# A three-block transformer kernel on one core: projection split, masked copies, norm gain and the order of a closing changed together

## The reference

```python
for layer in range(2):
    mix = dsa_mixer(h, ...) if layer == 0 else hgrn2_mixer(h, ...)
    h = layer_norm(ALPHA * h + mix, ...)
    h = layer_norm(ALPHA * h + swiglu(h, ...), ...)
# second block: rms norm, 16-head attention with relative bias, out-projection, gated conv feed-forward, rms norm
```

## Time and profile before

| what | us |
|---|---|
| median of 3 runs | 949.24 |
| lowest and highest run | 948.96, 949.47 |
| the profiled execution's own time | 951.03 |
| its span, first to last instruction | 949.0 |
| TensorE busy (matmul) in the span | 923.1 |
| VectorE busy | 590.3 |
| ScalarE busy | 457.8 |
| GpSimd busy | 156.0 |

### The profile page before, as it was taken

One profiled execution on the slowest core, in us unless ns is written; L12 is line 12 of the kernel. 1 busy time (PEld: TensorE's weight loads), 2 busy tenths in 40 slices (PEclk: granted clock), 3 DMA queues, 4 the chain that ended last, 5 costly groups with the idle time before them and its releaser, 6 DMA issues.

```text
span 949.0 us, 13816 instructions
## 1 busy us (share of the span) xinstructions
PE 923.1 (97%) x5667; PEld 760.8 (80%) x5667; DVE 590.3 (62%) x957; ACT 457.8 (48%) x609; POOL 156.0 (16%) x128
## 2 busy tenths in 40 slices
PE   8989999999999999899999999999999999999996
PEld 6867788888887997688888888878777788888885
DVE  5874774554648579978736456494223567777775
ACT  5775352433433443543425343345656465564653
POOL 3283300000005500013000000040355201010011
PEclk9999999999999999999999999999999999999999
DMA  8981466555646644245755555449432465555531
GB/s 292 208 163 46 148 228 198 179 179 192 204 143 217 221 147 166 92 131 178 245 178 179 192 199 185 164 158 320 133 134 89 155 207 185 185 178 178 180 130 45
DMA packets 104382, 164.98 MB, mean 174 GB/s; under 512 B 4011, under 2 KB 74714, under 8 KB 104320
## 3 DMA queue, kind: packets, MB, share of 16 engines
q1 hardware_dynamic: 101056, 152.61, 48.6%
q0 software_dynamic: 3264, 11.49, 5.6%
HBM read 159.89 MB, written 4.19 MB: 173 GB/s over the span
## 4 chain that ended last, share of the span: by engine, by line
PE 84%; DVE 8%; ACT 4%; DMA 1%; issue 1%; POOL 1%; SPq 0%; DVEq 0%; POOLq 0%; ACTq 0%
PE PG L1791 12%; PE PA L1791 12%; PE PG L1793 12%; PE PG L1792 12%; PE PA L1793 12%; PE PA L1792 11%; DVE wlo L600 1%; DVE work L1516 1%; ACT whi L591 1%; PE PG L1927 1%; PE TB L2379 1%; PE TB L2042 1%; PE TB L1947 1%; PE PA L2196 1%; PE PA L2195 1%
## 5 line engine op out<-in xcount | busy, mean ns | idle before, releaser
L600 DVE TENSOR_TENSOR wlo<-raw,whi 128x2048 fp32r<-128x2048 f32 (+1 forms) x124 | 288.9, 2346 | 65.5 <-ACT whi L591 65.4
L591 ACT ACTIVATE whi<-raw 128x2048 fp32r<-128x2048 f32 (+1 forms) x142 | 268.7, 1908 | 49.9 <-PE PA L1793 18.7
L1791 PE MATMUL PG<-whi,xlo 128*128 128x512 f32 x548 | 218.4, 399 | 0.3 <-DVE xlo L1098 0.2
L1793 PE MATMUL PG<-whi,xhi 128*128 128x512 f32 x548 | 214.1, 391 | 0.0
L1792 PE MATMUL PG<-wlo,xhi 128*128 128x512 f32 x548 | 213.9, 390 | 0.0
L1793 PEld LDWEIGHTS PG<-whi,xhi 128*128 128x128 f32 x548 | 103.1, 188 | 22.0
L1791 PEld LDWEIGHTS PG<-whi,xlo 128*128 128x128 f32 x548 | 103.2, 188 | 21.8 <-DVE wlo L1322 0.8
L1792 PEld LDWEIGHTS PG<-wlo,xhi 128*128 128x128 f32 x548 | 103.3, 189 | 20.1
L1791 PE MATMUL PA<-whi,xlo 128*128 128x512 f32 (+1 forms) x292 | 117.1, 401 | 1.8 <-DVE xlo L1098 1.3
L1793 PE MATMUL PA<-whi,xhi 128*128 128x512 f32 (+1 forms) x292 | 112.5, 385 | 0.0
L1792 PE MATMUL PA<-wlo,xhi 128*128 128x512 f32 (+1 forms) x292 | 112.2, 384 | 0.0
(11 more groups left out here) (289 smaller groups left out, 1175.3 us busy)
## 6 DMA issues: line engine op xcount, KB each, us to landing
raw<-in_ffn_w_gate SPq DMA_DIRECT2D x44, 512.0 KB, 4.0
raw<-in_ffn_w_up SPq DMA_DIRECT2D x44, 512.0 KB, 5.0
raw<-in_ffn_w_down SPq DMA_DIRECT2D x22, 1024.0 KB, 4.8
raw<-in_w_up SPq DMA_DIRECT2D x44, 512.0 KB, 4.6
raw<-in_hgrn_w_in SPq DMA_DIRECT2D x16, 1024.0 KB, 5.3
raw<-in_w_qkv SPq DMA_DIRECT2D x12, 1024.0 KB, 5.3
raw<-in_w_down SPq DMA_DIRECT2D x11, 1024.0 KB, 4.8
raw<-in_att_w_o SPq DMA_DIRECT2D x4, 1024.0 KB, 5.8
```

Of the source, the lines that this page charges most:

```text
L591: nc.scalar.activation(whi[:, g, 0:n_], raw[:, s, 0:n_], ACT.Copy).then_inc(S("w_hi"), 1)
L600: nc.vector.tensor_tensor(wlo[:, s, 0:n_], raw[:, s, 0:n_], whi[:, g, 0:n_].bitcast(F32), ALU.subtract).then_inc(S("w_lo"), 1)
L1791: mm(dst, xl[:, k, rows], whi[:, g, cols], start=first, stop=False)
L1793: return mm(dst, xh[:, k, rows], whi[:, g, cols], start=False, stop=last_)
```

## The change

It has six parts.

1. The first projection's units 0 and 1 carry columns 0 to 255 and 512 to 647 (392 columns, `FIRST`), unit 2 carries 256 to 511 (k and v whole, 256 columns).
2. The order of the beginning: the small constants are turned after the first and before the second half of iq; the query's turn comes ahead of them (event cq before c0); VectorE splits units 2 and 3 later; ScalarE takes the projection out before it rounds unit 3.
3. ScalarE rounds units U_AO+2 and U_AO+3 after pairs 2 and 4 instead of 0 and 1; U_F0+1 after the fourth group of outputs instead of before.
4. The first out-projection: tile 3 of U_AO+1 is left to between the closing's rows; tile 0 of U_AO+2 is done in the last pair; row 0 of the new h is turned inside row 1's last unit.
5. Masked copies take both heads of a bank and row at once.
6. The gain of the HGRN norm, now a value for each partition, scales the turned outputs in their rounding and split.

```diff
-SKIP, EARLY = 392, 256
-C_V, C_KI, C_WI, C_K = 248, 376, 504, 512
+EARLY, SKIP = 256, 512
+FIRST = EARLY + IN_COLS - SKIP
+C_KI, C_WI, C_K, C_V = 256, 384, 392, 520
...
-        for name, k in (("x", 4), ("c0", 2), ("cq", 1), ...
+        for name, k in (("x", 4), ("cq", 1), ("c0", 2), ...
...
+            def gained_hi(g):
+
+                e = ev["ho"] + g
+                turned(e)
+                act.wait_ge(S("gno"), 16)
+                ac.activation(flat(xhi[:, 2 * g:2 * g + 2, :]), TB[:, e % 2, :], ACT.Copy, scale=gno)\
+                  .then_inc(S("x_hi"), 1)
...
             hi(2)
-            hi(3)
-
-            act.wait_ge(S("ang"), 1)
-            ac.activation(trig.rearrange("p a b c -> p (a b c)"), ang.rearrange("p a b c -> p (a b c)"),
-                          ACT.Sin).then_inc(S("trig"), 1)
             full(1)
-            ac.activation(pin[:, :, 0:512], PG[:, :, :], ACT.Copy).then_inc(S("pin"), 1)
+            ac.activation(pin[:, :, 0:FIRST], PG[:, :, 0:FIRST], ACT.Copy).then_inc(S("pin"), 1)
...
-                if p < 2:
-                    hi(U_AO + 2 + p)
+                if p in (2, 4):
+                    hi(U_AO + 1 + p // 2)
                 if p == 5:
                     hi(U_F0)
-                if p == 7:
-                    hi(U_F0 + 1)
 
             attention("", probs_made)
             out_hi("", 3)
+            hi(U_F0 + 1)
+            x_hi_rows("n1", 0)
             hi(U_F0 + 2)
-            x_hi_rows("n1", 0)
             x_hi_rows("n1", 1)
...
-                        for c in range(2):
-                            ins = ve_.copy_predicated(dst[:, c], mk, src[:, c])
+                            mk = mk.unsqueeze(1).broadcast_to([P, 2, CHUNK >> i, m])
+                        else:
+                            mk = mk.unsqueeze(1).broadcast_to([P, 2, P])
+                        ins = ve_.copy_predicated(dst, mk, src)
...
-            vec.wait_ge(S("gno"), 16)
-            gv = flat(sg).rearrange("p (g c) -> p g c", c=DH)
-            link(ve_.tensor_tensor(gv, gv, gno.unsqueeze(1).broadcast_to([P, RT * HH, DH]), ALU.mult))
...
-            def closing(*units, between=None, begun=0, turn_next=None):
+            def closing(*units, between=None, begun=0, turn_next=None, first_row_tiles=(0, 1), row_1_first=None):
 
                 for r in range(RT):
+                    if r and row_1_first:
+                        row_1_first()
...
-                            for t in range(2):
+                            for t in range(2) if r or n_ else first_row_tiles:
...
             def turned_first(p):
-                if p >= 4:
+                if 4 <= p < 7:
                     out_tile(U_AO, "", (p - 4) // 2, 1 + 2 * (p % 2))
+                if p == 7:
+                    out_tile(U_AO, "", 2, 0)
...
-            out_closing(U_AO, "")
+            def second_unit():
+
+                for f in range(2):
+                    last = products(PA[:, 2 + f, :], 3, 1, U_AO + 1, slice(D + f * 512, D + (f + 1) * 512), False, False)
+                last.then_inc(S("w_used"), 1)
+
+            n1_ready = lambda r, g: pe.wait_ge(S("norm"), 2 * r + g + 1)
+            closing((U_AO + 2, 4, None, None, lambda r: parts_ready(turned_o[""][2])),
+                    (U_AO + 3, 6, None, None, lambda r: parts_ready(turned_o[""][3])),
+                    between=lambda: turn_out_rows("", 3), turn_next=lambda: turn_row_tile("n1", h, 0, n1_ready),
+                    first_row_tiles=(1,), row_1_first=second_unit)
```

More of the change, by code:

```diff
@@ L90, in weight_units @@
     v = w_in.rearrange("(t p) n -> p t n", p=P)
-    a = [[v[:, 4 * j:4 * j + 4, c:c + EARLY] for c in (0, SKIP)] for j in range(2)]
+    a = [[(0, v[:, 4 * j:4 * j + 4, 0:EARLY]), (EARLY, v[:, 4 * j:4 * j + 4, SKIP:IN_COLS])] for j in range(2)]
     a.append([(0, 8, SKIP - EARLY, v[:, :, EARLY:SKIP])])
@@ L758, in _ @@
             x_hi_rows("x", 0)
-            first, second = slice(0, UNIT // 2), slice(UNIT // 2, UNIT)
+            first, second = slice(0, 2 * FIRST), slice(2 * FIRST, 4 * FIRST)
             for u in range(2):
@@ L766, in _ @@
             hi(2)
+            full(1)
+            ac.activation(pin[:, :, 0:FIRST], PG[:, :, 0:FIRST], ACT.Copy).then_inc(S("pin"), 1)
+            act.wait_ge(S("pin"), 1)
+            for r in range(RT):
+                ac.activation(sq[:, r, :], pin[:, r, 0:NQL], ACT.Square,
+                              accum_out=ve[:, 8 + r:9 + r]).then_inc(S("ssq"), 1)
             hi(3)
@@ L1084, in lo_of_bank, with gained_lo @@
                    .then_inc(bank_free(e), 1)
-            def x_lo(name, parts=range(4)):
-                for g in parts:
-                    lo_of_bank(flat(xlo[:, 2 * g:2 * g + 2, :]), ev[name] + g, flat(xhi[:, 2 * g:2 * g + 2, :]))
+            def gained_lo(g):
+                e = ev["ho"] + g
+                nxhi[0] += 1
+                vec.wait_ge(S("x_hi"), nxhi[0])
+                vec.wait_ge(S("gno"), 16)
+                tiles = slice(2 * g, 2 * g + 2)
+                ve_.scalar_tensor_tensor(out=flat(xlo[:, tiles, :]), in0=TB[:, e % 2, :], scalar=gno,
+                                         in1=flat(xhi[:, tiles, :]).bitcast(F32), op0=ALU.mult, op1=ALU.subtract)\
+                   .then_inc(bank_free(e), 1)
             def x_lo_rows(name, r):
@@ L1318, in _ @@
             for u in range(2):
-                for part, made, done in ((slice(0, UNIT // 2), "first_hi", "first_lo"),
-                                         (slice(UNIT // 2, UNIT), "w_hi", "w_lo")):
+                for part, made, done in ((slice(0, 2 * FIRST), "first_hi", "first_lo"),
+                                         (slice(2 * FIRST, 4 * FIRST), "w_hi", "w_lo")):
                     vec.wait_ge(S(made), u + 1)
@@ L1373, in _ @@
             ins.then_inc(S("cqn"), 1)
+            lo(3)
+            lo_of_bank(flat(xlo[:, 0:2, :]), ev["cq"], flat(xhi[:, 0:2, :]))
+            e = ev["c0"]
+            turned(e)
+            ve_.tensor_copy(relT[0:BUCKETS, :], TB[0:BUCKETS, e % 2, 0:HQ]).then_inc(bank_free(e), 1)
             for r in range(RT):
@@ L1816, in turn_and_up @@
                                 parts_ready(ev[name] + 2 * r + k // 4)
[L1817 removed]
+                            n_ = 512 if u else FIRST
+                            last = products(bank(r)[:, 0:n_], k, r, u + s, slice(t * n_, (t + 1) * n_), k == 0, k == KT - 1)
                         if r == RT - 1:
@@ L2077, in later_columns @@
                     for r in range(RT):
-                        last = products(PA[:, 2 + r, 0:136], k, r, U_IN + 2, slice(k * 136, (k + 1) * 136), k == 0,
+                        last = products(PA[:, 2 + r, 0:256], k, r, U_IN + 2, slice(k * 256, (k + 1) * 256), k == 0,
                                         k == KT - 1)
@@ L2105, in _ @@
             lower, upper = lambda r: PA[:, r, :], lambda r: PA[:, 2 + r, :]
-            parts_ready(e)
+            pe.wait_ge(S("cst_loaded"), 96)
+            e = ev["c0"]
+            t_bank(e)
+            nc.tensor.transpose(TB[0:BUCKETS, e % 2, 0:HQ], relrow[0:HQ, :], ident[0:HQ, 0:HQ]).then_inc(S("t_full"), 1)
+            parts_ready(ev["cq"])
             pe.wait_ge(S("w_lo"), U_IQ + 1)
             halves(U_IQ, 0, lower).then_inc(S("iq_first"), 1)
+            t_bank(e + 1)
+            for j in range(4):
+                nc.tensor.transpose(TB[:, (e + 1) % 2, 44 * j:44 * j + 44], cw4[0:44, j, :], ident[0:44, 0:44])
+            last = nc.tensor.transpose(TB[:, (e + 1) % 2, 176:192], lbr[0:2 * HH, :], ident[0:2 * HH, 0:2 * HH])
+            last.then_inc(S("t_full"), 1)
+            parts_ready(e)
+            pe.wait_ge(S("pin"), 1)
+            mm(PG[0:HQ, 0, 0:T], relT[0:BUCKETS, :], hot[0:BUCKETS, :], start=True, stop=True).then_inc(S("reldist"), 1)
             e = ev["ki"]
```

75 lines of the change are left out of this document (23 added, 52 removed).

## The result

| | us, median (lowest to highest) |
|---|---|
| before, 6 runs | 949.41 (948.96 to 950.01) |
| changed, 6 runs | 954.52 (953.25 to 958.43) |

The ratio is 1.0057, with a 95% interval of 1.0046 to 1.0069: the change costs 5.1 us, 0.57%. The forecast was 951.6 us. The direction is right; the size is not, and 954.5 lies just outside the range.

The account below looks back on a forecast made before the run. TensorE, busy 97% of the span, bounds the kernel; VectorE the HGRN levels. The terms +5.1 + 1.4 - 0.6 - 0.4 - 2.6 - 0.5 = +2.4 us on 949.24 give 951.6 us, range 947.4 to 954.4.

Parts of the forecast that it names:

- 1a to 1d: Closing of the first attention: the product that starts at 109.64 starts at 114.7, +5.1 us, ends +4.3 and +5.6.
- (d): Closing: TensorE finishes row 1's products at 108.0, then waits 4.2 us at the turn of row 0.
- (c): Closing: the moved tile frees a buffer late; GpSimd's split runs 105.9 to 110.5, row 0's power behind it to 111.5.
- The clock term (+1.4): Closing: the 4.2 us wait should bring one fall of TensorE's clock, +1.4 us, ends 0 and 3.4.
- The rival of two falls: Closing: the clock falls twice, as two shorter waits come shortly before the long one; +2.0, 953.6 us; chance 0.12.
- waits (a) and (b): Closing: the replacement tile's products wait for xlo, 1.3 us later; then the last unit's row 0 starts 0.5 us later.
- The savings: The four parts outside the closing: roundings -0.6, projection -0.4, masked copies -2.6, norm gain -0.5 us.
- step 4: HGRN levels: half as many masked copies, 40 fewer at 0.07 us each; -2.6 us, ends -1.5 and -5.0.
- Step 3: Beginning: projection cut 392 + 256 columns, 1.9 us less work, only the rotation's second half gains; -0.4 us, ends +0.5 and -2.5.
- Step 2: First attention's heads: two roundings leave the chain, where they have 3.4 us; -0.6 us, ends 0 and -2.
- Step 5: HGRN norm: its gain leaves VectorE (2.28 us), but TensorE waits only 0.32 us there; -0.5 us, ends 0 and -2.3.
- The rival "GpSimd is not in the way": Closing: the power comes in time, so the closing costs some +0.6 us and no clock; 945.7 us, chance 0.13.

Follow-up runs that it names:

- e2: The changed kernel with the closing of the first attention as before, all else changed: 948.14 us, ratio 0.9987.
- e4: The changed kernel with row 0's turn inside row 1's last unit, but tile order and rounding of U_F0+1 as before: 947.08 us, ratio 0.9971.
- e8: The kernel of e4 with VectorE's split of the fifth weight unit moved between the two halves of qi's rotation: 947.32 us, ratio 0.9967.
- e6: The kernel before with the merged masked copies alone: 948.08 us, ratio 0.9978.
- e7: The kernel before with only the first projection's cut into 392 + 256 columns and the new order of the beginning: 950.21 us, ratio 1.0006.
- e10: The kernel before with only the two roundings moved from the first two pairs of heads to the third and fifth: 949.40 us, ratio 0.9993.
- e11: The kernel before with only the HGRN norm's gain made the scale of roundings and splits: 948.84 us, ratio 0.9986.
- e5: The changed kernel with GpSimd's row 0 power ahead of U_F0+1's split, which also waits for VectorE's second half of row 0's norm: 948.66 us, ratio 0.9990.

## Why the prediction was right and wrong

*The closing (1a to 1d) was right in mechanism and size.* The terms +5.1 and +1.4 make 6.5 us; the change against e2 is 6.4. The wait of (d) was forecast at 4.2 us and was 4.06. The split and the power of (c) start 0.6 us later than forecast, without a gap between them. Of the 7.2 us by which the next layer's first product is later, 5.1 are left without the clock, exactly the term.

*The clock term (+1.4) was low for the execution profiled*, where the fall begins only some 1 us ahead of the wait's end and lasts until behind 118 us. It took 2.1 us ahead of the next layer's first product and some 0.6 behind it. In the medians 6.4 - 5.1 = 1.3 us are left for it, close to the 1.4. That closeness is in part luck: the argument was that a 1.75 us wait had brought a fall, and the same wait brings none in e4 to e8. The rival of two falls, 953.6 us, was nearest to the result, for the wrong place: waits (a) and (b) brought no fall.

*The savings were too large, and this is the step that failed.* They were summed at -4.1 us and measured together at -1.3 (e2, interval -2.5 to 0), which is about the whole of the 2.7 us between +2.4 and +5.1. The largest error, 1.0 us, is in step 4: "Five levels with 8 copies less each: 40 x 0.07 = 2.8 us". The 0.07 came from two lengths, 2.20 us for 64 columns and 3.27 for 128, and was put on all five levels. Levels 0 and 1 had 2.47 and 2.45 us for the same 64 columns in the trace of before, which the earlier trace rows left out. Their copies are 0.153 us each instead of 0.138, and merged they take twice that, 0.309. In those levels the tensors are walked in runs of 1 and 2 columns. Three levels give 24 x 0.063 = 1.5 us. The low end that the prediction gave, -1.5, was the value.

The figure of 120 cycles from the Trainium skill, "VectorE: DVE Perf Modes", section on the TRN2 errata, would have made it 5.0 us. The prediction was right to keep to the spacings: e6 gave 1.6.

*Step 3, the projection (-0.4), was right on the first half of the rotation and wrong on the second.* The rotation did start at the place named (34.27 against "ends at 34.2"). But the gain of 0.4 us in the second half did not come, since ScalarE's copy of the scores released them: `[0.95 <-ACT work L807]`. The earlier trace rows had named the same releaser, with 0.34 us. e7 measured +0.5 us, interval -0.3 to +1.4, so this step is nearly as far off as step 4, 0.9 us, though less surely. e8 shows that the split in front was the hold, and that a part is lost again behind.

*Step 2, the roundings (-0.6), gave nothing that lasts.* e10 measured -0.2 us, and its interval, -1.5 to +0.2, would hold -0.6 too; its trace shows the gain of 1.1 us gone by the turn of h. What the prediction had as a caution took most of it: behind each rounding in its new place TensorE waits for a copy of probabilities, 0.41 and 0.35 us. The chain's 3.4 us were no measure of what leaves the path.

*Step 5, the norm gain (-0.5), was right* within the interval of e11, -2.3 to -0.4 us.

*The rival "GpSimd is not in the way"* was sound in its sum: it gave the closing +0.6 us in that case, and e5 against e2 is +0.5, though that difference is not clear of noise. What it lacked is that the power in time would not have been enough. Putting it ahead of the split, as e1 does, leaves 3.11 of the 4.06 us, since the split then stops VectorE.

## What to carry to other kernels

When a tile is moved behind another, ask which buffer it frees, who fills that buffer next, and what small step stands behind that filling in the same engine's order. A long GpSimd instruction on two SBUF operands is a hold for VectorE too, so on a critical stretch it is put where VectorE reads PSUM or waits anyway, or cut in pieces. A cost per instruction is read from the very shape that changes: two lengths of one shape say nothing of another with the same number of columns.
